# A recurrent stage rewritten: two PSUM banks per group, masks on GpSimd, products spread over the quarters of the array

## What is computed

```
def wkv_scan(state0, r, w, k, v, kk, a, reverse):
    def step(S, inp):
        r_t, w_t, k_t, v_t, kk_t, a_t = inp
        sa = jnp.einsum('bhij,bhj->bhi', S, kk_t)
        S = (S * w_t[:, :, None, :] - sa[..., None] * (kk_t * a_t)[:, :, None, :]
             + v_t[..., None] * k_t[:, :, None, :])
        return S, jnp.einsum('bhij,bhj->bhi', S, r_t)
    s_final, ys = lax.scan(step, state0, xs, reverse=reverse)
```

## Time and profile before

| | us |
|---|---|
| median of 3 runs (3493.92 to 3495.36) | 3493.93 |
| the profiled execution, its own time | 3495.4 |
| its span | 3493.6 |
| the recurrent stage, layer 1 and layer 2 | 261.5 and 264.5 |

### The profile page before, as it was taken

How to read it: one execution, slowest core, us unless ns; L and a number is a source line. 1 busy time by engine, 2 the same in 40 slices (tenths; PEclk the granted TensorE clock), 3 DMA queues, 4 the chain that set the end, 5 groups by cost and what they waited for, 6 DMA issues and landing times. The chain is left out here.

```text
span 3493.6 us, 68213 instructions
## 1 busy us (share of the span) xinstructions
PE 3330.0 (95%) x28698; PEld 2867.3 (82%) x28698; DVE 1858.0 (53%) x2801; ACT 1154.3 (33%) x1771; POOL 412.4 (12%) x280
## 2 busy tenths in 40 slices
PE   7999999999988899999999999999999978899999
PEld 5888888885668878888888888888895668789897
DVE  4552554665765555543554552554555765555353
ACT  3321222226652233321322331222226532234231
POOL 2000002004313211000002000002004233020000
PEclk9999999999999999999999999999999989999999
DMA  5222221440000012222221222221341000022222
GB/s 209 90 100 69 90 93 54 161 146 36 2 18 3 3 49 84 90 94 75 90 92 57 98 85 80 94 95 62 128 139 37 1 18 3 15 90 94 89 91 94
DMA packets 68294, 263.73 MB, mean 75 GB/s; under 512 B 7552, under 2 KB 8704, under 8 KB 67456
## 3 DMA queue, kind: packets, MB, share of 16 engines
q1 hardware_dynamic: 67664, 256.95, 21.9%
q10 hardware_dynamic: 432, 3.88, 0.3%
HBM read 258.70 MB, written 2.10 MB: 75 GB/s over the span
## 5 line engine op out<-in xcount | busy, mean ns | idle before, releaser
L240 PE MATMUL ps<-hn_hi,w_hi 128*128 128x512 f32 (+1 forms) x3520 | 864.3, 327 | 18.2 <-DVE hn_lo L457 5.9
L240 PE MATMUL ps<-hn_hi,w_lo 128*128 128x512 f32 (+1 forms) x3520 | 865.1, 327 | 0.0
L240 PE MATMUL ps<-hn_lo,w_hi 128*128 128x512 f32 (+1 forms) x3520 | 861.1, 326 | 0.0
L217 ACT ACTIVATE w_hi<-raw 128x1024 fp32r<-128x1024 f32 (+1 forms) x300 | 338.5, 1128 | 1376.8 <-PE ps L240 1224.1
L222 DVE TENSOR_TENSOR w_lo<-raw,w_hi 128x1024 fp32r<-128x1024 f32 (+1 forms) x300 | 396.8, 1323 | 470.8 <-ACT w_hi L217 463.4
L240 PEld LDWEIGHTS ps<-hn_hi,w_hi 128*128 128x128 f32 x3520 | 547.5, 190 | 82.7 <-issue 17.6
L240 PEld LDWEIGHTS ps<-hn_lo,w_hi 128*128 128x128 f32 x3520 | 548.2, 190 | 58.2
L240 PEld LDWEIGHTS ps<-hn_hi,w_lo 128*128 128x128 f32 x3520 | 545.0, 190 | 58.0
L240 PE MATMUL ps<-g_hi,w_hi 128*128 128x512 f32 (+1 forms) x1424 | 398.0, 347 | 6.1 <-DVE g_lo L894 6.1
L240 PE MATMUL ps<-g_lo,w_hi 128*128 128x512 f32 (+1 forms) x1424 | 403.6, 351 | 0.0
L240 PE MATMUL ps<-g_hi,w_lo 128*128 128x512 f32 (+1 forms) x1424 | 397.7, 347 | 0.0
(11 more groups left out here) (276 smaller groups left out, 4229.5 us busy)
## 6 DMA issues: line engine op xcount, KB each, us to landing
raw<-wgu SPq DMA_DIRECT2D x176, 512.0 KB, 3.5
w_mod_one<-wmod SPq DMA_DIRECT2D x100, 512.0 KB, 3.5
raw<-wdn SPq DMA_DIRECT2D x64, 704.0 KB, 4.0
raw<-win SPq DMA_DIRECT2D x44, 512.0 KB, 4.8
w_mod_two<-wmod SPq DMA_DIRECT2D x28, 512.0 KB, 3.7
w_mod_first<-wmod_first SPq DMA_DIRECT2D x4, 2048.0 KB, 22.5
raw<-wout SPq DMA_DIRECT2D x16, 512.0 KB, 3.5
h<-xT ACTq DMA_DIRECT2D x1, 3072.0 KB, 9.8
```

What stands on the lines that cost most here:

```text
L217: act.activation(w_hi[s][:, 0:kt, :].rearrange("p k n -> p (k n)"), raw[s][:, 0:kt * P], ACT.Copy).then_inc(hi_ready[s].sem, 1)
L240: mm = pe.matmul(out[:, o:o + b - a], w[:, k, :], m[:, k, a:b], start=(k == 0 and w is w_hi[s] and m is mov_hi), stop=(k == kt - 1 and w i ...
```

## The change

- `first_step`: level 0 and the transposed form come from the tensor engine out of a block that GpSimd has masked, 16 records by an identity and two products of 256 columns (four records) for each group. DVE adds the identity.
- `step_blocks`: GpSimd makes, for each round, six masked copies of the scores for each of three groups (18 operations of 128x256). The block product uses them, so that DVE no longer masks but only subtracts from the identity (`less_product`) and copies (`inverse_out`). The updated inverse is a whole product rather than a difference; ACT copies the transposed form (`transpose_out`, 15 a round).
- `block_product` and `step_products`: each group has a bank for either form (`BANK_X`, `BANK_XT`). The step products of one position go to (0,0), (1,1), (0,1), (1,0), that is, through all four quarters. At level 5 only one form is made, on two quarters. The score-and-value products ride in the block products of level 3 or 4, on the two quarters that those leave free.
- The turn of the values is made in forward rounds only; the copies of `b_nat` and `k_nat` go from ACT to DVE. `low_rank` is split in two calls, at level 1 and level 2.
- Chunk products in the order `QUADRANTS`; the two addend products per chunk move into the chain, straight into the state's bank, which removes the identity product, `s_add` and its copy. All states are kept, so outputs can come later (the first three at chunk 4). In the second layer outputs are made for the latent tokens alone.
- `y_loc` goes: DVE puts it into `y_sum`.

The diff's core (a forward/backward index such as `blocks_until` only counts semaphore steps):

```
+            def step_blocks(pool, r, li, g):
+                d = ROUNDS[r][1]
+                mask = masks[:, d, 5:6, :] if li == 0 else masks[:, 1 - d, 5 + li:6 + li, :]
+                pool.wait_ge(wkv_masked.sem, wkv_masked.at(r * NTT + 2 * g + 2))
+                pool.tensor_tensor(step_lo[li][:, of_group(g), :], sc[:, of_group(g), 0, :], mask.broadcast_to([P, UG, CH]),
+                                   ALU.mult).then_inc(lo_masked.sem, 1)
...
+                    def first_step(r, g):
+                        pe.wait_ge(lo_masked.sem, lo_masked.at(blocks_until(r, 0, g)))
+                        if g >= 1:
+                            pe.wait_ge(wkv_masked.sem, wkv_masked.at(r * NTT + NTT - 2 + g))
+                        for i, n in enumerate(units(g)):
+                            for b in range(2):
+                                pe.matmul(in_bank(BANK_X[g])[hr(b), i, :], step_lo[0][hr(b), n, :], K_["ident"][hr(b), hr(b)],
+                                          start=True, stop=True)
...
+                        for b in range(2):
+                            mm = pe.matmul(ps[hr(1 - b), BANK_XT[g], 0:UG * CH], K_["ident"][hr(b), hr(b)],
+                                           step_lo[0][hr(b), of_group(g), :].rearrange("p a b -> p (a b)"), start=True, stop=True)
...
+                    def block_product(r, li, g, values=False):
+                        pe.wait_ge(x_ready.sem, x_ready.at(r * STEPS + GROUPS * (li - 1) + g + 1))
+                        pe.wait_ge(lo_masked.sem, lo_masked.at(blocks_until(r, li, g)))
+                        for i, n in enumerate(units(g)):
+                            for b in range(2):
+                                mm = pe.matmul(in_bank(BANK_X[g])[hr(1 - b), i, :], step_lo[li][hr(b), n, :], x_inv[hr(b), n, :],
+                                               start=True, stop=True)
+                                if values:
+                                    mv = pe.matmul(slots[0][hr(b), n * CH:(n + 1) * CH], sc[hr(b), n, 2, :],
...
+                    def step_products(r, li, g):
+                        last = li == LEVELS - 1
+                        pe.wait_ge(t_ready.sem, t_ready.at(r * STEPS + GROUPS * (li - 1) + g + 1))
+                        if li >= 2:
+                            pe.wait_ge(xt_ready.sem, xt_ready.at(r * STEPS + GROUPS * (li - 2) + g + 1))
+                        for i, n in enumerate(units(g)):
+                            for b in (1, 0):
+                                mm = pe.matmul(in_bank(BANK_XT[g])[hr(b if last else 1 - b), i, :], lx[hr(1 - b), n, :],
+                                               xt_inv[hr(1 - b), n, :], start=True, stop=True)
+                            for b in (1, 0) if not last else ():
+                                mm = pe.matmul(in_bank(BANK_X[g])[hr(b), i, :], xt_inv[hr(1 - b), n, :], lx[hr(1 - b), n, :],
+                                               start=True, stop=True)
+                        mm.then_inc(step_ready.sem, 1)
...
+                        more = r + 1 < len(ROUNDS)
+                        for g in range(GROUPS):
+                            first_step(r, g)
+                        if r >= 1:
+                            pe.wait_ge(round_done.sem, round_done.at(r))
+                        else:
+                            pe.wait_ge(gate_tanh.sem, gate_tanh.at(2))
+                        if more:
+                            low_rank(r + 1, 0, slots[0])
+                        for g in range(GROUPS):
+                            block_product(r, 1, g)
+                        for g in range(GROUPS):
+                            step_products(r, 1, g)
+                        if more:
+                            pe.wait_ge(gate_tanh.sem, gate_tanh.at(2 * (r + 1) + 1))
+                            low_rank(r + 1, 1, slots[0])
...
+                        turn(r, 1)
...
+                        order = ORDER[d]
+                        for tt in range(NTT):
+                            for j, b in QUADRANTS:
+                                mm = pe.matmul(ps[hr(j), 2 + b, tt * CH:(tt + 1) * CH], neg_w[hr(b), 2 * tt + j, 0:64],
+                                               b_nat[hr(b), tt, hr(j)], start=True, stop=True)
+                        mm.then_inc(chunk_ready.sem, 1)
...
+                        def addends(i):
+                            tt, b = order[i] // 2, order[i] % 2
+                            for j in range(2):
+                                pe.matmul(state_bank(i)[hr(j), :], b_nat[hr(b), tt, hr(j)], neg_w[hr(b), 2 * tt + j, 64:128],
+                                          start=True, stop=False)
+                            for j in range(2):
+                                mm = pe.matmul(state_bank(i)[hr(j), :], k_nat[hr(b), tt, hr(j)], v_rw[hr(b), tt, hr(j)],
+                                               start=False, stop=i == 0)
+                            mm.then_inc((addends_ready if i else state_mm).sem, 1)
+                        addends(0)
+                        addends(1)
+                        for tt in range(OUT_TT):
                             cc = slice(tt * CH, (tt + 1) * CH)
-                            for j in range(2):
-                                n = 2 * tt + j
-                                pe.matmul(ps[hr(j), 2 + b, cc], neg_w[hr(b), n, 0:64], b_nat[hr(b), tt, hr(j)],
+                            for j, b in QUADRANTS:
+                                pe.matmul(ps[hr(j), 6 + b, cc], neg_w[hr(b), 2 * tt + j, 0:64], sc[hr(b), 2 * tt + j, 1, :],
                                           start=True, stop=True)
-                                pe.matmul(ps[hr(j), 4 + b, cc], b_nat[hr(b), tt, hr(j)], neg_w[hr(b), n, 64:128],
+                            for j, b in QUADRANTS:
+                                pe.matmul(ps[hr(j), b, cc], neg_w[hr(b), 2 * tt + j, 64:128], sc[hr(b), 2 * tt + j, 1, :],
                                           start=True, stop=False)
-                                mm = pe.matmul(ps[hr(j), 4 + b, cc], k_nat[hr(b), tt, hr(j)], v_rw[hr(b), tt, hr(j)],
+                            for j, b in QUADRANTS:
+                                mm = pe.matmul(ps[hr(j), b, cc], v_rw[hr(b), tt, hr(j)], sc[hr(b), 2 * tt + j, 3, :],
                                                start=False, stop=True)
                         mm.then_inc(chunk_ready.sem, 1)
...
+                        OUTPUTS_AT = {i: [i] for i in range(6, NCH)}
+                        OUTPUTS_AT.update({4: [0, 1, 2], 5: [3, 4, 5]})
+                        SCORES_AT = {2: 0, 3: 1, 5: 2, 6: 3, 8: 4, 9: 5}
...
+                        for i in range(1, NCH):
                             pe.wait_ge(state_ready.sem, state_ready.at(r * NCH + i + 1))
                             if i < NCH - 1:
+                                pe.wait_ge(addends_ready.sem, addends_ready.at(r * (NCH - 2) + i))
                                 for j in range(2):
-                                    mm = pe.matmul(ps[hr(j), 2 + i % 2, 0:CH], trans[hr(j), c, :], state[hr(j), i % 2, :],
+                                    mm = pe.matmul(state_bank(i)[hr(j), :], trans[hr(j), order[i], :], states[hr(j), i, :],
                                                    start=False, stop=True)
                                 mm.then_inc(state_mm.sem, 1)
...
-                                mm.then_inc(y_ready.sem, 1)
+                            for n in OUTPUTS_AT.get(i, ()):
+                                if n in with_output:
+                                    outputs(n)
-                            if r + 1 < len(ROUNDS) and i % 2 == 0:
-                                score_tile(r + 1, i // 2)
+                                addends(i + 1)
+                            if more and i in SCORES_AT:
+                                score_tile(r + 1, SCORES_AT[i])
...
+                    def inverse_out(r, li, g):
+                        dve.wait_ge(step_ready.sem, step_ready.at(r * STEPS + GROUPS * (li - 1) + g + 1))
+                        dve.tensor_copy(x_inv[:, of_group(g), :], in_bank(BANK_X[g])).then_inc(x_ready.sem, 1)
+                    def less_product(r, li, g):
+                        dve.wait_ge(lx_ready.sem, lx_ready.at(r * BLOCKS + GROUPS * li + g + 1))
+                        dve.tensor_tensor(lx[:, of_group(g), :], eye, in_bank(BANK_X[g]), ALU.subtract).then_inc(t_ready.sem, 1)
...
+                        for g in range(GROUPS):
+                            for li in range(LEVELS):
+                                step_blocks(pool, r, li, g)
```

More of the change, by code:

```diff
@@ new lines, in _, with free_of_turn @@
+                        turn(r, 1)
+                        for g in range(GROUPS):
+                            step_products(r, 2, g)
+                        def free_of_turn(i):
+                            pe.wait_ge(*nat_done(r, i))
+                        for li in (3, 4):
+                            values = li == 4 - d
```

(16 more changed lines are left out.)

406 lines of the change are left out of this document (197 added, 209 removed).

## The result

| | us |
|---|---|
| before, median (3491.87 to 3495.36) | 3493.93 |
| after, median of 4 runs (3407.91 to 3415.89) | 3414.72 |
| after, the profiled execution, its own time | 3415.9 |
| after, its span | 3414.1 |

The ratio is 0.9768, with a 95% interval of 0.9756 to 0.9780: 79 us less. The prediction said 3372 and 3347 to 3425. The time lies in the range, but not in the likeliest case: it is where the first rival, "records that can't start closer", had put it (3410 to 3432), 43 us above the forecast.

The account below looks back on a forecast made before the run. TensorE's streams of short records were taken as the bound, shortened by faster or fewer records. Round terms summed to 40.9 us; 133 gained over both layers less 11 for the clock gave 3373.4, median 3372, range 3347 to 3425.

Parts of the forecast that it names:

- the likeliest case: Four quarters run 64-column records at 0.0146 us, blocks and clock as assumed: 3372 (3355 to 3385), chance 0.52.
- the first rival: TensorE records can't start closer than about 0.026 us, so quarters bring nothing at 64 columns: 3410 to 3432, chance 0.27.
- The rates: TensorE records of 64 columns: 0.029 us each on two quarters, 0.0146 on four, by proportion from 128 columns.
- The sum: Middle round's terms added to 40.9 us against 57.37, a gain of 16.5; 133 over both layers, 122 after clock loss.
- First steps and the wait for GpSimd: Round's start: first steps 2.7 us, and TensorE waiting about 3 for the third group's first block, at 0.72 a block.
- the second rival: GpSimd sets the pace: blocks at 0.85 to 1.2 us lengthen TensorE's wait, 3386 to 3415, chance 0.12.
- the slower case: GpSimd blocks of over 2 us pace every round; at 2.3 us about 3527, slower than before, chance 0.03.
- Clock: One more fall of TensorE's granted clock per round, 1.4 us each, minus 11 over eight rounds.
- Level 5 with two turns: Level 5 makes one form on two quarters, 2.8 us against 4.06; remaining turns 2.2 in all, copy wait 0.5.
- Chunk products: Transition 0.7, two addends before the chain 0.4, outputs 2.1: together 3.2 us a round against 8.20 for 288 records.
- Chain: Round's end: 12 steps of 0.65 and its start, 8.4 us against 9.54, addends hidden in the 0.43 idle per step.
- The outputs left out in layer 2: Context outputs go in the second layer, 48 of 144 records and a third of those in the chain: 1 us a round.

Follow-up runs that it names:

- the run measured alone: Changed kernel plus five stretches of 768 identity-product records before layer 1's first score tiles; at 64 columns two quarters took 22.4 us, four in a loop 12.55.
- The undone quarters: Changed kernel with step products of levels 1 to 4 and all chunk products ordered so only two diagonal quarters work at a time: 3441.68 us, ratio 0.9840.
- the second profile: The changed kernel itself run once more, unaltered, beside the other runs on the same chip: 3418.83 us, ratio 0.9773 to the kernel before.
- run 64: The text names no run 64; 64 stands there only as a count of columns, records or products, so no change or time can be given.

## Why the prediction was off

The time lies within the range, but the likeliest case, from which the forecast comes, was wrong in one of its terms.

**What bounds the kernel.** Right for before: streams of short records. But "records that follow each other faster" was taken as the one thing that sets the pace, and the source of the records wasn't asked for.

**The rates.** Right: 0.0147 at four quarters and 64 columns, 0.0291 at two, in the run measured alone and in the kernel (96 step records in 1.63 us with the last one's end).

**The sum.** This is where it failed: at the step where 576 records of a round (384 of steps and 192 of chunk products) were multiplied by 0.0146 as if a burst's rate held for a whole round, and where the value products were put at no cost. A level's 144 records, with their waits, are 1.14 blocks, about 3.9 us in the mean at 3.45 a block, where the sum had 2.8. Levels 2 to 4 took 12.67 with a turn, not 9.1. A round's 2679 instructions are 10.5 blocks, 36 us at that pace, which the forecast's 40.9 respects. But where TensorE waits or works on long products a block takes 5 us and more (10.7 at GpSimd's wait), and the dense blocks behind can't make up for it. The forecast for the rounds was 133 less 11, and 84 came: of the 38 that lack, 25 are visible stalls. The undone quarters put the whole loss to the supply at 35, of which 15 are inferred. The rival's 672 records were miscounted: the values leave 48 and not 96.

**First steps and the wait for GpSimd.** 5.22 against 5.7, with a wait of 2.4 against 3. Over all rounds it was 13.1 and not 24, since the first round of either layer has none. A block took 0.73 us (median) against the 0.72 taken:

```profile
L1795 POOL TENSOR_TENSOR step_lo<-sc,masks x144: 712/728/2192, 1022.4 to 2927.6; 128x256 f32<-128x256 f32 x144
```

The pieces of 64 and the repeated mask cost nothing that shows, so the second rival and the slower case fell with their premise. The argument against them was misread, though: only the growth from row to row is 2.1 ns a column, the rows themselves are 1.9 to 2.5, and a block takes 2.8.

**Clock.** The half-rate gate products and level 1 cost 1.6 + 1.4 us in this round, against the 1.4 allowed. Over all eight rounds it is the other way round: the time at the lower level rose from 20 to 31 us (35 in the second profile), which costs at most 5 to 7 us, against the 11 allowed. So the clock explains none of the 38 that lack. The 0.80 over level 1 before was two fifths of that stretch at the lower level, and not half.

**Low-rank** 2.6 forecast, 2.85 + 1.48 measured, the first call at half clock. **Level 5 with two turns** 4.8 forecast (2.8, two of the three turns and 0.5), 6.32 measured with a stall of 1.45. **The inverse times a_mv** 3.5, measured 3.53. **Chunk products** 3.2, measured 3.10: right, behind a stretch of few, long records (a block of 5.8 us), in which the next block had time to come. **Chain** 8.4, measured 9.32: the addends were to hide in the hand-overs; the copies of the state start 0.66 to 1.65 us apart, where the kernel before had 0.65 to 0.79 from the second one on, and the blocks there are 3.4 to 4.4 us long, so this stretch too is near the supply, which no run here separates from the score tiles' own time. **The outputs left out in layer 2**, 4 us: the run that made them again couldn't tell.

**The rival.** It named the right number, 0.026 us as the closest that records came in any long run, and the right total, but as a limit on each start. Starts 0.0147 apart are seen everywhere; it is the block that can't be had faster, 3.45/128 = 0.027. That the two numbers lie so close is chance, and so is it that its total came out. The floor of 25 ns from start to start that the Trainium skill states in "TensorE: Matmul & The Clock Gate" (Wait — 56ns, not 53.3ns?) doesn't hold for these products on four quarters: in the loop records start 16.3 ns apart in the mean over 768.

## What to carry to other kernels

Ask of a speed-up by faster short instructions where they come from: in straight-line code 256 TensorE instructions (64 fp32 products) took 3.45 us here in a long dense run, and less only for two or three blocks behind a slower one. So once a product of such a run goes faster than 0.054 us, only fewer instructions or a loop can help. No run here put the rounds into a loop. Gaps put down to "issue" that stand a fixed number of instructions apart are its mark. And a wait in front of dense short work can cost twice, by itself and by the clock behind it (0.50 and 0.67 in the second round): the order in which a helper engine makes its parts should follow who needs them first, which here was worth 24 us for a table of 18 entries.

## What the runs showed of the hardware

- One block of 256 TensorE instructions took 3.45 us in a run alone, and 3.0 to 4.7 us (median 3.6) in the rounds where it ended in a stall. The packet of 16 KB took 0.9 to 1.4 us in the records, started 0.6 to 2.4 us after the first instruction of the block before, and landed 1.2 to 1.6 us before TensorE went on.
- A loop of 192 instructions turns in 0.15 us over its work; 8 turns came with one packet.
- Four quarters keep 0.0147 us a record at 64 columns; two 0.0291.
